# Token-major projections of a hybrid mixer: twelve tiles of 512 columns in place of sixteen of 384

## The reference

```python
h = rms_norm(x, norm_g)
z = h @ w_in                      # columns: qa 384, ka 128, va 128, qr 384, kr 384, vr 384, gr 384, up 256
ya = sliding_window_attention(qa, ka, va, sinks, rel_bias)   # window 128, sinks, bias by distance
yr = retention(qr, kr, vr, gr)    # rotary on q and k, chunks of 128, per-head norm, swish gate
yp = pool_mixer(up, pool_w, pool_scale)
x = x + concat(ya, yr, yp) @ w_out
x = x + relu(rms_norm(x) @ w_up) ** 2 @ w_down
out = rms_norm(x)
```

## Time and profile before

| | us |
|---|---|
| median of 3 runs (2020.38 to 2020.73) | 2020.39 |
| span of the profiled execution | 2018.4 |
| TensorE busy | 2006.9 (99%) |
| VectorE busy | 1416.2 (70%) |
| ScalarE busy | 891.2 (44%) |
| GpSimd busy | 190.9 (9%) |
| one token-major stage (second quarter, 235.96 to 316.34) | 80.4 |

### The profile page before, as it was taken

How to read it: one execution, slowest core, us unless ns; L and a number is a source line. 1 busy time by engine, 2 the same in 40 slices (tenths; PEclk the granted TensorE clock), 3 DMA queues, 4 the chain that set the end, 5 groups by cost and what they waited for, 6 DMA issues and landing times.

```text
span 2018.4 us, 26877 instructions
## 1 busy us (share of the span) xinstructions
PE 2006.9 (99%) x9964; PEld 1691.7 (84%) x9964; DVE 1416.2 (70%) x2043; ACT 891.2 (44%) x1500; POOL 190.9 (9%) x279
## 2 busy tenths in 40 slices
PE   9999999999999999999999999999999999999998
PEld 8988898889889888888888888888888888888886
DVE  6685578558746977777778677677666668667667
ACT  5433543543354426545456544445333334433333
POOL 2042113203220330000000000000000000000001
PEclk9999999999999999999999999999999999999999
DMA  8133412522252233676856566787957578756572
GB/s 285 56 98 136 142 63 74 193 84 79 100 181 85 93 117 102 149 185 160 181 149 152 136 154 179 178 190 198 396 196 276 197 298 323 287 202 261 200 289 84
DMA packets 101950, 348.64 MB, mean 173 GB/s; under 512 B 10267, under 2 KB 12220, under 8 KB 84412
## 3 DMA queue, kind: packets, MB, share of 16 engines
q1 hardware_dynamic: 99372, 338.27, 52.6%
q10 hardware_dynamic: 2448, 8.65, 1.2%
HBM read 270.21 MB, written 76.68 MB: 172 GB/s over the span
## 4 chain that ended last, share of the span: by engine, by line
PE 98%; DVE 1%; ACT 1%; issue 0%; POOL 0%; POOLq 0%; ACTq 0%
PE bank L2145 30%; PE bank L2147 30%; PE bank L2146 30%; PE bank L2242 1%; PE bank L2270 1%; PE bank L2318 1%; PE bank L2299 1%; PE bank L2321 1%; PE bank L2285 1%; PE bank L2361 1%; PE bank L2326 1%; PE bank L2256 1%; DVE hT_lo L1443 1%; PE bank L2346 0%; PE bank L2135 0%; PE bank L2336 0%
## 5 line engine op out<-in xcount | busy, mean ns | idle before, releaser
L2145 PE MATMUL bank<-h_hi,w_lo 128*128 128x512 f32 x912 | 355.7, 390 | 0.2 <-DVE h_lo L1654 0.2
L2147 PE MATMUL bank<-h_hi,w_hi 128*128 128x512 f32 x912 | 354.9, 389 | 0.0
L2146 PE MATMUL bank<-h_lo,w_hi 128*128 128x512 f32 x912 | 354.9, 389 | 0.0
L2145 PE MATMUL bank<-d_hi,u_lo 128*128 128x512 f32 x896 | 348.5, 389 | 0.0
L2146 PE MATMUL bank<-d_lo,u_hi 128*128 128x512 f32 x896 | 348.5, 389 | 0.0
L2147 PE MATMUL bank<-d_hi,u_hi 128*128 128x512 f32 x896 | 348.5, 389 | 0.0
L1286 ACT ACTIVATE u_hi<-u_raw 128x1024 fp32r<-128x1024 f32 x112 | 118.5, 1058 | 327.7 <-PE bank L2147 315.2
L1906 DVE TENSOR_TENSOR u_lo<-u_raw,u_hi 128x1024 fp32r<-128x1024 f32 x112 | 137.1, 1224 | 179.6 <-ACT u_hi L1286 179.6
L2145 PE MATMUL bank<-ring_hi,hT_lo 128*128 128x384 f32 (+1 forms) x672 | 241.3, 359 | 0.0
L2147 PE MATMUL bank<-ring_hi,hT_hi 128*128 128x384 f32 (+1 forms) x672 | 234.1, 348 | 0.0
L2146 PE MATMUL bank<-ring_lo,hT_hi 128*128 128x384 f32 (+1 forms) x672 | 233.8, 348 | 0.0
(11 more groups left out here) (220 smaller groups left out, 3109.0 us busy)
## 6 DMA issues: line engine op xcount, KB each, us to landing
u_raw<-u_dram SPq DMA_DIRECT2D x56, 1024.0 KB, 4.8
d_raw<-in_wdn SPq DMA_DIRECT2D x56, 1024.0 KB, 6.9
stage<-in_wmix SPq DMA_DIRECT2D x108, 512.0 KB, 4.4
u_dram<-ur SPq DMA_DIRECT2D x32, 1280.0 KB, 9.7
wraw<-in_wup SPq DMA_DIRECT2D x128, 256.0 KB, 3.8
e_raw<-in_wdn SPq DMA_DIRECT2D x24, 1024.0 KB, 8.9
xq<-in_x SPq DMA_DIRECT2D x16, 512.0 KB, 3.6
x_dram<-xq ACTq DMA_DIRECT2D x16, 512.0 KB, 3.0
```

Of the source, the lines that this page charges most:

```text
L2145: pe.matmul(dst, al, bh, start=(first and k == 0), stop=False, skip_group_check=chain)
L2146: pe.matmul(dst, ah, bl, start=False, stop=False, skip_group_check=chain)
L2147: last = pe.matmul(dst, ah, bh, start=False, stop=(final and k == n - 1), skip_group_check=chain)
```

## The change

The 1536 token-major columns are cut into three groups of 512 in place of four of 384. A group has four weight units of two chunks x 512 columns (in place of three units of 8 chunks x 128), and four token blocks: 12 tiles a quarter of 8 chunks x 3 matmuls of 512 columns. `proj_G` now takes steps, one chunk of one tile each; a round is 12 steps (a tile and a half), and the insertions stand after 6 of them, in odd rounds and some even ones in the middle of a tile. The first two units of a group are released half way through its last tile, by a new semaphore `half_tile_done`. Splits, tanh, rotation and gates move between the rounds; GpSimd's `rot_b(b)` waits for tile 4+b. The number of tiles goes from 39 to 35, and with it the bank of each output tile turns.

```diff
-T_GROUP, T_UP1, T_OA, T_OR, NT = 6, 22, 23, 31, 39
+T_GROUP, T_UP1, T_OA, T_OR, NT = 6, 18, 19, 27, 35
+GSTEPS = C * (T_UP1 - T_GROUP) // 8
-        return T_GROUP + 4 * ((u - 6) // 3) + 3
+        return T_GROUP + NB * ((u - 6) // 4) + 3
-SLOT = [3, 4, 5, 0, 1, 2] + 2 * [3, 4, 5, 0, 1, 2] + [4, 5, 3, 0, 1, 2, 4, 5, 0]
+SLOT = 3 * [0, 1, 2, 3, 4, 5] + [1, 0, 2, 3, 4, 5, 1, 2, 3]
+def released_half_way(u):
+    return 6 <= u < 18 and (u - 6) % 4 < 2
...
@@ GpSimd, rot_b
                 if b == 0:
...
-                    evacuated(pool, q, T_GROUP + 7)
+                evacuated(pool, q, T_GROUP + NB + b)
@@ ScalarE, split_hi
-                    act.wait_ge(tile_done.sem, tile_done.now(q, last_tile_of_unit(owner)))
+                    if released_half_way(owner):
+                        act.wait_ge(half_tile_done.sem, half_tile_done.now(q, (owner - 6) // 4))
+                    else:
+                        act.wait_ge(tile_done.sem, tile_done.now(q, last_tile_of_unit(owner)))
@@ ScalarE, evac_G
-                act.activation(zt[:, b, 384 * g:384 * g + 384], dense[(T_GROUP + t) % 3][:, 0:384],
+                act.activation(zt[:, b, 512 * g:512 * g + 512], dense[(T_GROUP + t) % 3][:, :],
@@ ScalarE, the rounds
                 for i in range(8):
-                    evac_G(q, 2 * i)
+                    if i % 2:
+                        evac_G(q, 3 * (i // 2) + 1)
+                    if i == 2:
+                        split_hi(q, 12)
+                        split_hi(q, 13)
                     if i in (2, 4, 6):
                         yA_high(q, i // 2 - 1)
+                    if i == 5:
+                        split_hi(q, 16)
+                        split_hi(q, 17)
+                    if i == 7:
+                        tanh_of(q, 1)
+                        split_hi(q, 20)
+                        split_hi(q, 21)
                     if i < 7:
                         exps(q, i + 1)
-                    evac_G(q, 2 * i + 1)
-                    if i % 2 == 1:
-                        for u in range(3):
-                            split_hi(q, 12 + 3 * (i // 2) + u)
-                    if i in (5, 6):
-                        tanh_of(q, 2 * (i - 5))
-                        tanh_of(q, 2 * (i - 5) + 1)
+                    evac_G(q, 3 * (i // 2) + 2 * (i % 2))
+                    if i == 3:
+                        split_hi(q, 14)
+                        split_hi(q, 15)
+                    if i == 6:
+                        split_hi(q, 18)
+                        split_hi(q, 19)
+                        tanh_of(q, 0)
+                split_hi(q, 22)
+                split_hi(q, 23)
+                tanh_of(q, 2)
+                tanh_of(q, 3)
                 yA_high(q, 3)
                 evac_qkT(q, 0)
@@ VectorE, the rounds
                     softmax(q, i)
+                    if i in (2, 5):
+                        split_lo(q, 12 if i == 2 else 16)
+                        split_lo(q, 13 if i == 2 else 17)
...
-                    if i in (2, 4):
-                        for u in range(3):
-                            split_lo(q, 9 + 3 * (i // 2) + u)
+                    if i == 3:
+                        split_lo(q, 14)
+                        split_lo(q, 15)
+                    if i == 4:
+                        rot_a(q, 0)
+                        rot_add(q, 0)
                     if i == 5:
-                        for b in range(2):
-                            rot_a(q, b)
-                            rot_add(q, b)
+                        rot_a(q, 1)
+                        rot_add(q, 1)
                     if i == 6:
-                        gate_of(q, 0)
-                        gate_of(q, 1)
                         rot_a(q, 2)
                         rot_add(q, 2)
                         split_lo(q, 18)
                         split_lo(q, 19)
                     if i == 7:
+                        gate_of(q, 0)
                         rot_a(q, 3)
                         rot_add(q, 3)
                         evac_pt(q, 7)
-                        gate_of(q, 2)
-                        gate_of(q, 3)
+                        gate_of(q, 1)
                         split_lo(q, 20)
+                        split_lo(q, 21)
                         pool_first(q, 0)
                         pool_rest(q, 0)
-                for u in range(21, 24):
-                    split_lo(q, u)
+                split_lo(q, 22)
+                split_lo(q, 23)
+                gate_of(q, 2)
+                gate_of(q, 3)
                 evac_scaled(q, T_UP1)
@@ TensorE
-                ev, k = evac_of(t - 3 if t >= 3 else t - 3 + NT)
+                ev, k = evac_of(t - 3 if t >= 3 else NT - 1 - (NT - 1 - t) % 3)
+            def proj_G(q, first_step, last_step):
+                for step in range(first_step, last_step):
+                    t, c = divmod(step, C)
+                    g, b = divmod(t, NB)
+                    if c == 0:
+                        free_bank(q, T_GROUP + t)
+                    if b == 0 and c % 2 == 0:
+                        pe.wait_ge(wlo_done.sem, wlo_done.now(q, 6 + 4 * g + c // 2))
+                    s, cols = SLOT[6 + 4 * g + c // 2], slice(512 * (c % 2), 512 * (c % 2) + 512)
+                    tok = slice(b * P, (b + 1) * P)
+                    last = three(dense[(T_GROUP + t) % 3][:, :],
+                                 [(hT_hi[:, c, tok], hT_lo[:, c, tok], ring_hi[:, s, cols], ring_lo[:, s, cols])],
+                                 first=(c == 0), final=(c == C - 1))
+                    if c == C - 1:
+                        last.then_inc(tile_done.sem, 1)
+                    elif b == NB - 1 and c == C // 2 - 1:
+                        last.then_inc(half_tile_done.sem, 1)
...
                 for i in range(8):
-                    proj_G(q, 2 * i)
+                    proj_G(q, GSTEPS * i, GSTEPS * i + GSTEPS // 2)
                     if i in (2, 4, 6):
                         att_out(q, i // 2 - 1)
                     if i < 6:
                         att_scores(q, i + 2)
-                    proj_G(q, 2 * i + 1)
+                    proj_G(q, GSTEPS * i + GSTEPS // 2, GSTEPS * i + GSTEPS)
                     att_transposes(q, i)
```

More of the change, by code:

```diff
@@ L276, in build @@
         tile_done = Events(sem("tile_done"), NT)
+        half_tile_done = Events(sem("half_tile_done"), 3)
         z_evac = Events(sem("z_evac"), T_OA - len(SCALED))
@@ L1019, in evac_G @@
                 act.wait_ge(tile_done.sem, tile_done.now(q, T_GROUP + t))
-                g, b = t // 4, t % 4
+                g, b = divmod(t, NB)
                 act.wait_ge(rstd_done.sem, rstd_done.now(q, b))
-                act.activation(zt[:, b, 384 * g:384 * g + 384], dense[(T_GROUP + t) % 3][:, 0:384],
+                act.activation(zt[:, b, 512 * g:512 * g + 512], dense[(T_GROUP + t) % 3][:, :],
                                ACT.Copy, scale=rstd[:, b:b + 1]).then_inc(z_evac.sem, 1)
@@ L2130, in _ @@
             for e in (rbmm_done, tile_done, vtr_done, s_done, ptr_done, o_done, qktr_done, rs_done, ro_done, ru_done,
-                      ytr_done, mix_done):
+                      ytr_done, mix_done, half_tile_done):
                 pe.sem_inc(e.sem, e.primed)
@@ L2451, in direct_product @@
                         if i == 0:
+                            pe.wait_ge(x2_evac.sem, x2_evac.now(NQ - 1, 14))
+                        elif i == 1:
                             pe.wait_ge(x2_evac.sem, x2_evac.now(NQ - 1, 13))
-                        elif i == 1:
-                            pe.wait_ge(x2_evac.sem, x2_evac.now(NQ - 1, 15))
                         elif i == 2:
@@ L2460, in direct_product @@
                         if n == 1:
-                            pe.wait_ge(x2_evac.sem, x2_evac.now(NQ - 1, 14))
+                            pe.wait_ge(x2_evac.sem, x2_evac.now(NQ - 1, 15))
                         else:
@@ L2615, in layout_mixer_weights @@
     cols += [s + np.arange(P) for s in (ka, va, up)]
-    cols += [s + c * P + np.arange(P) for s in (qr, kr, gr, vr) for c in range(3)]
     cols += [up + P + np.arange(P)]
     units = [w_in[:, k].reshape(C, P, P).transpose(1, 0, 2).reshape(P, C * P) for k in cols]
+    group = np.concatenate([s + np.arange(3 * P) for s in (qr, kr, gr, vr)]).reshape(3, 512)
+    units[6:6] = [w_in[2 * P * i:2 * P * i + 2 * P, k].reshape(2, P, 512).transpose(1, 0, 2).reshape(P, 1024)
+                  for k in group for i in range(4)]
     rows = [pair[c] for c in range(GROUP)] + [384 + c * P + np.arange(P) for c in range(5)]
```

## The result

| | us |
|---|---|
| before, median of 17 runs (2020.24 to 2021.37) | 2020.62 |
| changed, median of 17 runs (2023.38 to 2024.87) | 2024.21 |
| ratio, 95% interval | 1.0017 [1.0010, 1.0023] |
| forecast on the first median | 2023.3 |

The changed kernel is 3.6 us slower, where +2.9 was forecast. The interval leaves out 1, so the slowdown is small but clear of the noise. TensorE's busy time in the page fell from 2006.9 to

What follows compares the result with a forecast made beforehand. The prediction took TensorE's full queue as the bound. Wider matmuls (-5.4 us) and four new waits (+8.3 us) summed to +2.9 us on the 2020.4 us median, giving 2023.3 us, range 2017.0 to 2026.5.

Steps and rivals of the forecast that it cites:

- The reading of the bound: Whole kernel: TensorE, busy 2006.9 of 2018.4 us with nearly no stall; time is a sum of its start-to-start intervals.
- Part 2: Round 4 of each quarter: att_out(1) waits for evac_pt(3), 2.07 us, four times, 8.3 us lost.
- X: Start of the last matmul of group tile 5, the end of round 3; att_out(1) is due at X+4.76.
- The turns: After round 3: GpSimd's two products and VectorE's two split_lo alternate instruction by instruction; evac_pt(3), reading PSUM, is not held.
- The upper bound: Wait at att_out(1): 2.6 us a quarter, with one more GpSimd product in front.
- Part 1: Token-major group: 1152 matmuls of 512 columns replace 1536 of 384, at 226.7 against 173.5 ns, 5.4 us less.
- a switch costs as before: TensorE's insertions between dense matmuls: no added cost from the widening, at most 0.1 us x 32 either way.
- Units 16 and 17: Weight units released half way in tile 7: low parts ready with 0.45 and 0.7 us to spare, no cost.
- Y: Start of tile 7's last matmul; low parts of units 16 and 17 were put at Y+3.33 and Y+4.47.
- The end of the stage: Two tanh ahead of evac_qkT(0) on ScalarE, before ret_scores(0): 0.3 us of spare kept, no cost.
- C: Rival: no wait shows at all, 2015.0 us; chance 0.10.
- D: Rival: spare at units 16 and 17 lost, tile 8 waits 0.4 to 1.2 us a quarter, 2024.9 to 2028.1; chance 0.20.

Runs made afterwards that it cites:

- e2: The changed kernel, with GpSimd's rot_b(1) also waiting for evac_pt(3), so its products do not run beside split_lo(14) and (15): 2020.03 us, ratio 0.9996.
- e3: The changed kernel, with GpSimd's rot_b(1) done twice, four products where there were two: 2024.04 us, ratio 1.0018.
- e1: The changed kernel, with split_lo(14) and split_lo(15) moved on VectorE behind evac_pt(3) and softmax(4) in round 4: 2017.01 us, ratio to before 0.9982.
- e7: e1, with the scores of rounds 0 and 1 moved straight ahead of the transposes: 2016.11 us, ratio to before 0.9979.
- e8: e1, with GpSimd's rot_b(2) done twice, so its products still run when split_lo(16) and (17) are issued: 2017.64 us, ratio to before 0.9986.
- e4: The changed kernel, with split_lo(15) alone moved behind evac_pt(3), split_lo(14) staying in round 3: 2016.97 us, ratio 0.9982.
- e5: The changed kernel, with split_hi(14) and (15) moved on ScalarE ahead of exps(4) in round 3: 2016.93 us, ratio 0.9983.
- e6: The changed kernel, with split_hi(14) and (15) moved on ScalarE between exps(4) and evac_G(5): 2016.74 us, ratio 0.9981.

## Why the prediction was right

**The reading of the bound** held: TensorE's queue is full, and the change is worth its intervals less its new holes.

**Part 2, the wait at `att_out(1)`.** Right in place and cause, and near in number: 4 times, behind pt. 2.07 us were forecast, 1.82 came (X+6.58 against X+6.83). Half of the 0.25 is one input: GpSimd started at X+1.19 and not X+1.35, 0.07 after the evacuation's end where its one row of before showed 0.23, so its first product was over 0.12 sooner. That row was rot_b(0)'s; in the changed kernel rot_b(0) and (2) also start 0.23 behind the evacuation in every quarter, and only rot_b(1) 0.08. Why it is shorter there stays open. The other half is small change: 0.09 over the three held instructions, 0.04 at the handover from pt to `att_out`. No step of the chain was off by more than 0.06 beside that start: `evac_G(5)` came at X+0.43 with 0.69, split_lo at X+2.09 for 2.11. The turns, read off, are borne out by the changed kernel's own rows; e2 shows what they cost (without them 0.6 us of idle, as against 0.74 in the bounds), and e3 that more products behind add nothing. The upper bound, 2.6 a quarter for one more product in front, is not what its own numbers give: 2.07 and a product of 1.16 make 3.2. No run came near it.

**Part 1, the widening**, is the term that was mis-sized: 5.4 us forecast, 3.9 in the traces. Summed over the dense runs of the stage, each to the next instruction, the kernel before takes 275.5 us and e1 271.6. The step that failed is "a switch costs as before". Late in a run the intervals are 173.3 and 226.7 ns in both traces; the 173.5 of the earlier trace rows is the mean over 17 intervals that hold a few slower ones, and this alone puts 0.3 us too much into the term. Counted above these two intervals, the 60 dense runs cost 9.3 us before and 10.5 in e1, so the switches took back 1.2:

| dense runs behind | number | before, us above 173.3 ns each | e1, us above 226.7 ns each |
|---|---|---|---|
| transposes | 32 | 5.5 | 6.4 |
| scores | 24 | 3.3 | 3.4 |
| `att_out` | 4 | 0.5 | 0.7 |

The first interval behind a switch is about 0.1 us longer at both widths. The difference comes after it: with 512 columns some five more intervals are 228 to 236 ns, 232 in the mean (about ten are slow behind the transposes of v and behind `att_out`), while with 384 columns they are at 173.3 at once behind transposes, and slow only behind scores (174.6 in the mean over 22 intervals, where 512 columns have 228.3 over 16). The bound of 0.1 us x 32 that was kept for the switches covers it. e7 shows one switch as a whole, 0.14 us, where it is taken away; but it is a switch from scores, at which the two widths lose the same, so e7 does not isolate what was missing. Why a tail stands behind transposes with 512 columns and not with 384 stays open.

The errors, 1.0 too much for the wait and 1.5 too much for the gain, nearly cancel in the sum: 8.3 - 5.4 = 2.9 against 7.26 - 3.93 = 3.3. That the sum came closer than either term is luck. The prediction also said that a change under 0.2% can't be told from none; the intervals of this study can do it, for the changed kernel as for e1.

**The waits that cost nothing** did so. Units 16 and 17: the first was ready at 295.03 + 1.22, 3.32 behind Y (292.94) where 3.33 was worked out, and no matmul of round 5 waited. The end of the stage: the copies for `ret_scores(0)` were done at 328.28, scores began 328.67, 0.4 us of spare where 0.3 was left. ScalarE there, answering to the earlier trace rows:

```profile
325.26 1.06 ACT L968 ACTIVATE ring_hi<-stage 128x1024 fp32r<-128x1024 f32 x1 [4.96 <-DMA stage<-in_wmix]
326.22 0.92 ACT L1071 ACTIVATE thb<-zt 128x384 f32<-128x384 f32 x2
327.05 0.47 ACT L1049 ACTIVATE yA_hi<-bank 128x384 fp32r<-128x384 f32 x1
327.42 0.86 ACT L1062 ACTIVATE sc<-bank 128x384 f32<-128x384 f32 x2
```

**The rivals.** C (no wait) did not come, since VectorE's own chain exceeds the 4.76 us, as e2 shows with GpSimd out of the way. D did not come by itself; e8 had to double a block of GpSimd's to bring it, and then it cost 0.2 us a quarter, below the 0.4 to 1.2 put on it.

## What to carry to other kernels

Where one engine's queue is full, list for each instruction in it the last producer, and walk that producer's own queue: the loss here was a VectorE copy that was itself ready on time, but stood behind two weight splits whose input another engine had queued behind the very matmul that ended the round. When tiles grow wider and rounds shorten, splits that used to be fed early can become fed at the round's end; either the consumer (e1, e4) or the producer (e5, e6) may be moved, and each of them turned a loss of 3.6 us into a gain of as much. Take the interval of a matmul from runs of the same length between switches, not from an undisturbed stretch.

## What the runs showed of the hardware

- VectorE and GpSimd products with SBUF inputs exclude each other and here alternated one by one: two split_lo against two products 3.49 in place of 2.36, and the same 3.49 against four products (e3, with the limit told there). The Trainium skill, page "SBUF — State Buffer", section "Who interferes with whom", says that a VectorE instruction with two SBUF inputs contends with a GpSimd instruction that reads SBUF; these rows agree, and the copy from PSUM with the window mask kept its 1.01.
- After a switch from short matmuls to 512-column ones, the first interval is 0.32 to 0.34 us and the next five or so 0.228 to 0.236, before 0.2267 is reached. 384-column matmuls go back to 0.173 at once after transposes, but not after scores (0.171 to 0.185 for some eight intervals). I had not expected a tail.
- It is not only VectorE's two-input products that are held. In the kernel before, softmax's three scalings by 1/sum stood beside the four products of the earlier trace rows and took 3.25 us, where the changed kernel's at 283.81 take 0.68; the products kept their 1.16 each:

```profile
278.65 3.25 DVE L1499 TENSOR_SCALAR sc<-sc,rinv 128x128 f32<-128x128 f32 x3
```
